# Gate rows of the first 128 tokens: one fp32 product per token becomes two fp32r products on a one-hot table split into high and low halves

## The reference, cut to what matters

```python
act = jax.nn.gelu(jnp.einsum('td,thkd->thk', xc, u[ec]), approximate=False)
return jnp.einsum('thk,thkd->td', gc * act, v[ec])
```

## Time and profile before

| | us |
|---|---|
| median of 3 runs | 2848.39 |
| lowest and highest | 2843.57, 2848.76 |
| the profiled execution | 2854.08 |
| its span in the trace | 2852.3 |
| TensorE busy | 2745.3 (96%) |
| DVE busy | 2240.2 (79%) |
| ACT busy | 1158.3 (41%) |

### The profile page before, as it was taken

The page is one execution under the profiler, slowest core; times in us unless marked ns, Lnnn a source line. Parts: engine busy times, 40 slices in busy tenths (PEclk is TensorE's granted clock), DMA queues, the critical chain, the costliest instruction groups (busy, mean ns, idle before and its releaser), DMA issues.

```text
span 2852.3 us, 51149 instructions
## 1 busy us (share of the span) xinstructions
PE 2745.3 (96%) x19786; PEld 2489.3 (87%) x19786; DVE 2240.2 (79%) x4318; ACT 1158.3 (41%) x1664; POOL 570.6 (20%) x354
## 2 busy tenths in 40 slices
PE   6999999999999999999999999999999999999998
PEld 6998787899999997787899987788999999977776
DVE  7998676579977658888789986766889766688887
ACT  4533421244444443333355343222444444433334
POOL 0000002120877630000000000030227677100000
PEclk9999999999999999999999999999999999999999
DMA  7553451455888778878745534444568887788785
GB/s 294 184 187 119 152 188 36 163 225 196 220 226 242 202 226 296 283 282 281 250 150 185 172 109 179 132 133 154 182 202 216 244 224 202 254 288 291 280 284 195
DMA packets 258985, 593.81 MB, mean 208 GB/s; under 512 B 82608, under 2 KB 198064, under 8 KB 200240
## 3 DMA queue, kind: packets, MB, share of 16 engines
q1 hardware_dynamic: 192656, 572.74, 58.0%
q0 software_dynamic: 36864, 0.15, 2.8%
q10 hardware_dynamic: 29216, 17.57, 2.1%
HBM read 537.27 MB, written 53.08 MB: 207 GB/s over the span
## 4 chain that ended last, share of the span: by engine, by line
PE 76%; DVE 12%; DMA 6%; ACT 3%; issue 2%; POOL 0%; SPq 0%; DVEq 0%; ACTq 0%; POOLq 0%
PE ps L1191 25%; PE ps L1170 15%; PE ps L684 13%; PE ps L646 6%; DMA act_rows<-region 5%; DVE u_lo L2104 2%; PE ps L1180 2%; PE ps L774 2%; PE ps L1056 2%; PE ps L724 1%; PE ps L933 1%; DVE region L1713 1%; DMA ring<-in_stream 1%; ACT u_hi L1505 1%; PE ps L1003 1%
## 5 line engine op out<-in xcount | busy, mean ns | idle before, releaser
L1170 PE MATMUL ps<-h_hi,u_hi 128*128 128x256 f32 x2048 | 589.4, 288 | 13.1 <-DVE u_lo L2104 12.4
L1170 PE MATMUL ps<-h_lo,u_hi 128*128 128x256 f32 x2048 | 579.1, 283 | 0.0
L1170 PE MATMUL ps<-h_hi,u_lo 128*128 128x256 f32 x2048 | 578.9, 283 | 0.0
L2352 POOL DMA_INDIRECT gate_rows<-route x256 | 478.6, 1870 | 294.2 <-DVE route L2218 134.0
L2104 DVE TENSOR_TENSOR u_lo<-ring,u_hi 128x1024 fp32r<-128x1024 f32 x256 | 312.7, 1222 | 210.5 <-ACT u_hi L1505 194.1
L1170 PEld LDWEIGHTS ps<-h_hi,u_hi 128*128 128x128 f32 x2048 | 392.2, 191 | 20.5 <-DVE u_lo L2104 19.8
L1170 PEld LDWEIGHTS ps<-h_lo,u_hi 128*128 128x128 f32 x2048 | 392.6, 192 | 0.0
L1170 PEld LDWEIGHTS ps<-h_hi,u_lo 128*128 128x128 f32 x2048 | 392.2, 192 | 0.0
L1526 ACT ACTIVATE u_hi<-ring 128x1024 fp32r<-128x1024 f32 x192 | 203.9, 1062 | 324.3 <-PE ps L1191 324.3
L2111 DVE TENSOR_TENSOR u_lo<-ring,u_hi 128x1024 fp32r<-128x1024 f32 x192 | 235.0, 1224 | 51.9 <-ACT u_hi L1526 51.7
L1533 ACT ACTIVATE region<-ps 128x256 f32<-128x256 f32 x256 | 98.2, 383 | 429.0 <-DMA act_rows<-region 230.5
(11 more groups left out here) (394 smaller groups left out, 5191.2 us busy)
## 6 DMA issues: line engine op xcount, KB each, us to landing
ring<-in_stream SPq DMA_DIRECT2D x456, 1024.0 KB, 7.6
act_rows<-region SPq DMA_DIRECT2D x256, 128.0 KB
gate_rows<-rstd ACTq DMA_DIRECT2D x2, 8192.0 KB, 29.7
region<-gate_rows SPq DMA_DIRECT2D x256, 64.0 KB, 4.0
region<-act_rows SPq DMA_DIRECT2D x128, 128.0 KB, 4.2
small_inverse<-act_rows SPq DMA_DIRECT2D x128, 128.0 KB, 4.2
gate_rows<-route POOLq DMA_INDIRECT x256
region<-in_c SPq DMA_DIRECT2D x7, 512.0 KB, 5.7
```

The lines of the kernel that those rows point to most:

```text
L1170: ins = mm(ps[:, c % 4, 0:T], x, y[:, k, :], start=k == 0 and i == 0, stop=k == KD - 1 and i == 2)
L2352: gp.indirect_dma_start(gate_cells, bass.IndirectOffsetOnAxis(ap=gate_at[:, r:r + 1].bitcast(I32), axis=0), gate_weight[:, r:r + 1], None, ...
```

## The change

Each one-hot product of the first half of the tokens becomes two products of type fp32r that accumulate in the same PSUM columns. The row table holds zeros and ones, which fp32r holds exactly; it is stationary in both. The gates are split once per layer into `weight_hi`, rounded to fp32r, and `weight_lo`, the rest; one column table is made with each.

```diff
+        hot_hi, hot_lo, hot_row = over(hot_at, "hot_hi", 0, 8, P), peer("hot_lo", 31744, 8, P), over(hot_at, "hot_row", 1024, 8, P)
+        weight_hi, weight_lo = sb("weight_hi", [P, P], F32R), sb("weight_lo", [P, P])
...
                     for t in range(4):
                         i = (4 * s + t) % 8
-                        ins = mm(ps[:, 4 + s % 4, t * P:(t + 1) * P], hot[:, 1, i, :], hot[:, 0, i, :], start=True, stop=True)
+                        o = ps[:, 4 + s % 4, t * P:(t + 1) * P]
+                        mm(o, hot_row[:, i, :], hot_hi[:, i, :], start=True, stop=False)
+                        ins = mm(o, hot_row[:, i, :], hot_lo[:, i, :], start=False, stop=True)
                     ins.then_inc(S["gates_mm"], 1)
...
-                    vec.tensor_tensor(hot[:, 1, at_ring:at_ring + 4, :], keys, mine, ALU.is_equal)
-                    for t in range(4):
-                        ins = vec.tensor_scalar(hot[:, 0, at_ring + t, :], K("iota"), route[:, 0, first + t:first + t + 1],
-                                                route[:, 2, first + t:first + t + 1], ALU.is_equal, ALU.mult)
+                    vec.tensor_tensor(hot_row[:, at_ring:at_ring + 4, :], keys, mine, ALU.is_equal)
+                    for there, weight in ((hot_hi, weight_hi[:, :].bitcast(F32)), (hot_lo, weight_lo)):
+                        for t in range(4):
+                            ins = vec.tensor_scalar(there[:, at_ring + t, :], K("iota"), route[:, 0, first + t:first + t + 1],
+                                                    weight[:, first + t:first + t + 1], ALU.is_equal, ALU.mult)
                     ins.then_inc(S["hot_ready"], 1)
...
                 dve.wait_ge(S["route_copied"], 1)
+                ch.join(vec.tensor_copy(weight_hi[:, :], route[:, 2, 0:P]))
+                ch.join(vec.tensor_tensor(weight_lo[:, :], route[:, 2, 0:P], weight_hi[:, :].bitcast(F32), ALU.subtract))
                 for c in range(GATE_AT, CHUNKS):
```

## The result

The median rose from 2848.39 us to 2859.38 us; the ratio to the kernel before is 1.0033, with a 95% interval of 1.0020 to 1.0046, so between 6 and 13 us slower, 9.4 us at the ratio itself. One of the seven executions, 3620.84 us at a granted clock of 0.70, is outside that ratio, which compares fast executions alone. The forecast was +6.0 us, 2854.4 us.

What follows compares the result with a forecast made beforehand. TensorE was taken to bound the gate steps. +1.4 (TensorE) + 2.0 + 2.4 + 0.2 (waits for DVE's tables) = +6.0 us on 2848.4 gave 2854.4 us; own range 2849 to 2864, with the faster rival 2822 to 2864.

Steps and rivals of the forecast that it cites:

- What bounds: Gate steps: TensorE always busy, 0.89 us a step in a 6.64 us period, 57 us at stake over 64 steps.
- TensorE's part: Gate step's eight records: each fp32r record takes 0.114 us, held by its weight load; +1.4 us over 64 steps.
- (a): Gate step's fp32r records go by moving columns, 0.47 us a step: 2826 us in all; chance 0.17.
- (b): Narrow fp32r product as slow as a full fp32 one, +57 us at the gate steps: 2907 us; chance 0.15.
- DVE in the steady period: Most gate steps: four more TENSOR_SCALAR cost 1.02 us, slack shrinks from 2.04 to 1.02 us, no cost to TensorE.
- DVE where there is no slack: Gate steps whose tables come late make TensorE wait: +2.0, +2.4 and +0.2 us.
- the two first steps: First gate step of each layer, where TensorE already waits for tables: 1.02 us more each, +2.0 us.
- steps behind gate_ada: Eight gate steps after gate_ada's extra reductions, slack 0.49 to 1.6 us: only the tightest overrun, +0.2 us.
- other late steps: Gate steps right behind a u_hi that waited for a store: half of 4.8 us taken, +2.4 us.
- the six late ones: Six gate steps beside the two first ones, three a layer, listed with under 1.02 us between tables and TensorE's loads.
- (c): Same record floor, but TensorE's lateness is made up at the next store wait: 2851 us; inside the forecast's 0.68.
- The split of the gates: Two DVE instructions a layer and their joins, under 1 us, hidden before a u_lo for which DVE idles 3.14 us.

Runs made afterwards that it cites:

- the run with 64 columns: The changed kernel with each fp32r product of 128 moving columns made as two of 64: 2907.12 us in a single execution.
- DVE's work alone: The kernel before with four more TENSOR_SCALAR a step, written to a table nobody reads, fp32 products kept: 2859.3 us, ratio 1.0030.
- the one with the stores moved: The changed kernel with SP's two stores of activations put before the wait and load of the next block: 2834.28 us, ratio 0.9949.

## Why the prediction was right

**What bounds.** Right: TensorE's time of a step goes into the end, and the loss is waits of TensorE.

**TensorE's part.** The floor was right, and so, as far as the rows go, was its cause, the load of 128 stationary columns, read from a fp32 line with 2 moving columns and from equal load durations. The record was put at 0.108 to 0.120 us and taken as 0.114; it is 0.111. The term was +1.4 us and is 0. Rivals (a), a record that goes by its columns, and (b), a fp32r product as slow as a fp32 one, both fell with the 6.64 us period; the run with 64 columns shows directly that the moving columns don't matter there.

**DVE in the steady period.** Right: eight TENSOR_SCALAR in a row, a slack of 0.8 to 1.0 us at most steps and no wait there. The added four move DVE's next instruction by 1.02 us, as priced:

```profile
871.73 1.31 DVE L2237 TENSOR_SCALAR hot_lo<-cst,route,weight_lo 128x128 fp32r<-128x128 f32 x4
872.75 1.22 DVE L2108 TENSOR_TENSOR u_lo<-ring,u_hi 128x1024 fp32r<-128x1024 f32 x1
```

At half of the steps their end, for which TensorE waits, comes 0.2 us later than that.

**DVE where there is no slack.** The three terms added up to 4.6 us, and the waits grew by 6.9 us. This was the weakest step. Its terms against the two traces with DVE's added work:

| | priced | changed kernel | DVE's work alone |
|---|---|---|---|
| the two first steps | +2.0 | +0.25 | +2.0 |
| steps behind gate_ada | +0.2 | +2.25 | +2.0 |
| other late steps | +2.4 | +4.4 | +2.9 |

The first steps came out as priced in one trace and hardly moved in the other: there the tables of the first layer came 0.76 us later than before (832.69 against 831.93), but TensorE had come 0.97 us later too (each time less its wait, 831.36 against 830.39). What was mis-sized in both is the term of gate_ada. The prediction's own figures did not give 0.2 us: 1.02 us of own work and up to 0.8 us pushed in, against slacks of 0.49 to 1.6 us, allow an overrun at each of the eight steps. One of these steps, with 0.49 us, also stood in the list of the six late ones, so it was counted twice; and the step at 2344.39 stood there with 0.06 us of slack, since its wait of 0.47 us was not taken off. Of the six, the changed kernel pays at two, 0.49 us (873.09) and 1.98 us (2337.95), and the run with DVE's work alone at the three of the second layer, 1.04, 1.00 and 0.67 us. The list was of one execution; which chunks meet a late store changes as soon as anything moves. That the terms gave a sum near the measured one is in part luck: +1.4 us for TensorE was 0, and gate_ada's 0.2 us was ten times that. By the ratio the time rose by 9.4 us, 3.4 us more than forecast and inside the stated 2849 to 2864 us.

**What the prediction left out.** It said that no DMA is moved and did not follow DVE's lateness past u_lo. SP's load waits for u_lo, two stores wait behind that load, and ACT waits for a store: DVE's time can come back to DVE, as in the rounds from 916 to 958 us. Case (c), that a late TensorE meets the next store with more slack and gets its time back, would have given 2851 us; the two runs with DVE's added work gave 2859 us, and the one with the stores moved shows that the lateness of the stores is needed for any loss at all, behind gate_ada too. How much of the loss is the loop's feedback was not measured by itself.

**The split of the gates.** Right: 0.22 and 0.29 us, hidden before a u_lo for which DVE still idles 1.22 us at 828.56.

## What to carry to other kernels

Splitting a product into cheaper ones saves nothing when each piece reloads the same 128 stationary columns and moves few: a record of 128 moving columns cost 0.111 us here in either type, and one of 64 in fp32r no less. So make the split halves one wide moving operand (0.118 us for both) and pay for the addition instead. A work item added to an engine with a third of its time idle is free or not by what its lateness reaches: follow it through every queue that waits on it, SP's too. Stores that are ready should not stand behind a load that waits; here that order alone was worth 15 us, and it hid the change's DVE work completely.

## What the runs showed of the hardware

With 128 stationary columns and the granted clock at 1.00, the spacing of matmul records was 0.111 us for fp32r with 64 and with 128 moving columns and for fp32 with 128, 0.108 us for fp32 with 2, 0.118 us for fp32r with 256 and 0.2345 us with 512. That 64 and 128 columns give the same number, in a type for which no such row was there before, was not certain beforehand. With 256 moving columns a fp32 record took 0.216 us (3.46 us for 16, line 774 in the earlier trace rows), and a fp32 product is two records: by these spacings two fp32r products take about half the time there, and at 128 columns nothing of that is left.

TENSOR_SCALAR of 128 elements start 0.26 us apart, with fp32 and with fp32r output alike. The four that come second in a step are busy for 76.9 us over 64 steps against 71.7 us for the first four, and in the run with fp32 tables, where the two groups write the memories the other way round, 77.2 against 71.7 us. So neither the type nor the place of the table makes the difference. It is mostly in the last of the eight, which lasts 0.53 us in 31 of the 64 steps of the changed kernel and 0.34 us in the others; why is open.
